# Low weight parts by an adding transfer in place of a GpSimd subtraction, and low products last in each unit

## The reference

```
for l in range(2):
    h = rmsnorm(x, norm_g[l])
    u_a, z_a, u_b, z_b, q, z_x, g_a, g_b, g_x = split(h @ w_in[l])     # 1024 x 7168
    y_a = s5_branch(u_a) ; y_a = y_a * sigmoid(y_a @ w_glu + b_glu)
    o_a = (y_a * silu(z_a)) @ w_br_ssm
    c_b = silu(layernorm(conv31(u_b[:, :512] * sigmoid(u_b[:, 512:]))))
    o_b = (c_b * silu(z_b)) @ w_br_conv
    o_x = (attention(q, memory) * silu(z_x)) @ w_br_xatt
    m = sigmoid(g_a) * o_a + sigmoid(g_b) * o_b + sigmoid(g_x) * o_x
    x = x + m @ w_out
y = rmsnorm(x, final_norm_g)
```

## Time and profile before

| | us |
|---|---|
| median of 3 runs | 1299.31 (1298.57 to 1300.8) |
| profiled execution, device time | 1295.11 |
| profiled execution, span of its instructions | 1293.3 |
| TensorE busy | 1163.0 (90%), 8322 matmuls |
| VectorE busy | 833.9 (64%) |
| ScalarE busy | 395.3 (31%) |
| GpSimd busy | 387.6 (30%), of which L555 366.0 |
| DMA engines, mean busy share | 37.5% |

### The profile page before, as it was taken

The page is one execution under the profiler, slowest core; times in us unless marked ns, Lnnn a source line. Parts: engine busy times, 40 slices in busy tenths (PEclk is TensorE's granted clock), DMA queues, the critical chain, the costliest instruction groups (busy, mean ns, idle before and its releaser), DMA issues.

```text
span 1293.3 us, 19959 instructions
## 1 busy us (share of the span) xinstructions
PE 1163.0 (90%) x8322; PEld 1068.3 (83%) x8322; DVE 833.9 (64%) x1223; ACT 395.3 (31%) x556; POOL 387.6 (30%) x183
## 2 busy tenths in 40 slices
PE   5997999979788987989999979999979798979995
PEld 4497989579788987989977968868969798969995
DVE  1889964888779860457825995757857887233322
ACT  4331433142242423223214234233314241312212
POOL 0144234233231432133321522322343222304340
PEclk8998999999897998989999989999989799989998
DMA  7563235732121255154334623547221214422442
GB/s 202 164 226 99 63 115 158 139 88 65 53 82 33 66 121 132 38 134 158 108 99 133 210 64 99 179 126 111 82 68 54 62 35 119 98 66 87 132 131 66
DMA packets 205808, 137.94 MB, mean 107 GB/s; under 512 B 45842, under 2 KB 186570, under 8 KB 204934
## 3 DMA queue, kind: packets, MB, share of 16 engines
q1 hardware_dynamic: 205574, 135.61, 37.5%
q10 hardware_dynamic: 144, 1.05, 0.2%
HBM read 121.86 MB, written 15.72 MB: 106 GB/s over the span
## 4 chain that ended last, share of the span: by engine, by line
PE 67%; DVE 19%; DMA 4%; ACT 3%; SPq 3%; issue 2%; POOL 1%; DVEq 0%; ACTq 0%
PE acc L635 46%; DVE cacc L1363 9%; PE acc L676 4%; PE acc L981 3%; PE mp L831 2%; PE mp L888 2%; PE mp L600 2%; PE mp L764 1%; DMA w_st<-in_w_in 1%; DVE X L1357 1%; PE mp L690 1%; POOL w_lo L555 1%; DVE t L1357 1%; PE mp L805 1%; PE mp L855 1%
## 5 line engine op out<-in xcount | busy, mean ns | idle before, releaser
L555 POOL TENSOR_TENSOR w_lo<-w_st,w_hi 128x1024 fp32r<-128x1024 f32 x144 | 366.0, 2542 | 852.3 <-ACT w_hi L1068 852.0
L635 PE MATMUL acc<-h_hi,w_hi 128*128 128x260 f32 x1664 | 345.4, 289 | 7.6 <-DVEq L1691 7.6
L1068 ACT CAST w_hi<-w_st 128x1024 fp32r<-128x1024 f32 x144 | 150.9, 1048 | 643.7 <-PE acc L635 602.0
L635 PE MATMUL acc<-h_lo,w_hi 128*128 128x260 f32 x1664 | 337.4, 285 | 0.0
L635 PE MATMUL acc<-h_hi,w_lo 128*128 128x260 f32 x1664 | 337.2, 285 | 0.0
L635 PEld LDWEIGHTS acc<-h_hi,w_hi 128*128 128x128 f32 x1664 | 260.6, 191 | 14.5 <-issue 10.0
L635 PEld LDWEIGHTS acc<-h_hi,w_lo 128*128 128x128 f32 x1664 | 259.1, 190 | 0.0
L635 PEld LDWEIGHTS acc<-h_lo,w_hi 128*128 128x128 f32 x1664 | 258.9, 190 | 0.0
L1363 DVE SCALAR_TENSOR_TENSOR cacc<-vx,cw,cacc 128x512 f32<-128x512 f32 x232 | 220.1, 1019 | 3.0 <-DVE xT L1357 1.5
L635 PE MATMUL acc<-bh,w_hi 128*128 128x260 f32 x384 | 85.7, 307 | 32.4 <-ACTq L1201 13.2
L635 PEld LDWEIGHTS acc<-bh,w_hi 128*128 128x128 f32 x384 | 64.9, 207 | 35.6 <-issue 17.3
(11 more groups left out here) (276 smaller groups left out, 1481.4 us busy)
## 6 DMA issues: line engine op xcount, KB each, us to landing
w_st<-in_w_in SPq DMA_DIRECT2D x104, 512.0 KB, 3.9
kb<-in_cache_mem_k SPq DMA_DIRECT2D x16, 512.0 KB, 5.7
kb<-in_cache_mem_v SPq DMA_DIRECT2D x16, 512.0 KB, 4.1
w_st<-in_w_out SPq DMA_DIRECT2D x16, 512.0 KB, 4.1
x_scratch<-xT SPq DMA_DIRECT2D x8, 520.0 KB, 6.8
xT<-x_scratch SPq DMA_DIRECT2D x4, 1040.0 KB, 8.0
kvw<-in_w_k SPq DMA_DIRECT2D x8, 512.0 KB, 6.5
kvw<-in_w_v SPq DMA_DIRECT2D x8, 512.0 KB, 3.6
```

Of the source, the lines that this page charges most:

```text
L555: pool.tensor_tensor(w_lo[:, n % 2, :], w_st[:, n % 2, :], w_hi[:, n % 2, :].bitcast(F32), ALU.subtract).then_inc(w_staged_free, 1)
L635: last = pe.matmul(acc_ps[acc][:, a, 0:HC], w_of(w, slot, k), x_of(x, k, a), start=(k == 0 and p == 0), stop=(k == kts - 1 and p == 2))
L1068: act.copy(w_hi[:, n % 2, :], w_st[:, n % 2, :]).then_inc(w_hi_done, 1)
```

## The change

`w_lo` is made in another way and used at another time.

- ACT, right after it rounds `w_hi`, waits for that copy and writes its negative into `w_lo` (a second pass over 128 x 1024).
- GpSimd no longer computes. It issues a transfer that adds `w_st` onto `w_lo` in SBUF, so that `w_lo` holds `w_st - w_hi`. The landing is told by one semaphore for each slot, `w_lo_done[0]` and `w_lo_done[1]`.
- SP's next load into the slot waits for that landing.
- TensorE begins a unit when `w_hi` is there (`w_hi_done`). It does all products with `w_hi` first, and those with `w_lo` last, behind a wait for the landing.

```
-            w_staged_free = sem("w_staged_free")
+            w_lo_done = [sem(f"w_lo_done{i}") for i in range(2)]
             w_hi_done = sem("w_hi_done")
+            w_neg_done = sem("w_neg_done")
...
             def ring_load(l, src, i, width=P):
                 n = l * UNITS + i
-                sp.wait_ge(w_staged_free, n + 1)
+                if n >= 2:
+                    sp.wait_ge(w_lo_done[n % 2], 16 * (n // 2))
                 sp.dma_start(w_st[:, n % 2, :]...).then_inc(w_loaded[n % 2], 16)
...
-            pool.sem_inc(w_staged_free, 2)
...
                 def low(name, first, end):
-                        pool.wait_ge(w_hi_done, n + 1)
-                        pool.tensor_tensor(w_lo[:, n % 2, :], w_st[:, n % 2, :], w_hi[:, n % 2, :].bitcast(F32),
-                                           ALU.subtract).then_inc(w_staged_free, 1)
+                        pool.wait_ge(w_neg_done, n + 1)
+                        pool.dma_start(w_lo[:, n % 2, :], w_st[:, n % 2, :], accum_op=ALU.add).then_inc(w_lo_done[n % 2], 16)
...
-            def products(l, slot, acc, name, i, terms, kts, x_of, w_of, tiles_done=None):
+            def products(l, n, acc, name, i, high, low, kts, w_of, tiles_done=None):
+                pe.wait_ge(w_hi_done, n + 1)
                 wait(pe, l, f"acc_free{acc}", use[name] + i + 1)
                 for k in range(kts):
                     if tiles_done:
                         wait(pe, l, tiles_done, k + 1)
-                    for p, (w, x) in enumerate(terms):
+                    for x in (high, low):
                         for a in range(2):
-                            last = pe.matmul(acc_ps[acc][:, a, 0:HC], w_of(w, slot, k), x_of(x, k, a),
-                                             start=(k == 0 and p == 0), stop=(k == kts - 1 and p == 2))
+                            pe.matmul(acc_ps[acc][:, a, 0:HC], w_of(w_hi, n % 2, k), x[:, k, a, :],
+                                      start=(k == 0 and x is high), stop=False)
+                pe.wait_ge(w_lo_done[n % 2], 16 * (n // 2 + 1))
+                for k in range(kts):
+                    for a in range(2):
+                        last = pe.matmul(acc_ps[acc][:, a, 0:HC], w_of(w_lo, n % 2, k), high[:, k, a, :],
+                                         start=False, stop=(k == kts - 1))
                 last.then_inc(acc_ready[acc], 1)
...
     in high(n), on ACT:
                     act.copy(w_hi[:, n % 2, :], w_st[:, n % 2, :]).then_inc(w_hi_done, 1)
+                    act.wait_ge(w_hi_done, n + 1)
+                    act.activation(w_lo[:, n % 2, :], w_hi[:, n % 2, :].bitcast(F32), ACT.Copy, scale=-1.0).then_inc(w_neg_done, 1)
```

More of the change, by code:

```diff
@@ L640, in tile_w @@
                 return w[:, slot, k * P:(k + 1) * P]
-            def tile_x(x, k, a):
-                return x[:, k, a, :]
             def in_unit(l, name, i, tiles_done=None):
                 n = l * UNITS + unit[name] + i
-                pe.wait_ge(w_staged_free, n + 3)
-                products(l, n % 2, i % 2, name, i // 2, ((w_hi, h_hi), (w_lo, h_hi), (w_hi, h_lo)), KT, tile_x, tile_w, tiles_done)
+                products(l, n, i % 2, name, i // 2, h_hi, h_lo, KT, tile_w, tiles_done)
             def gate(l, name, j):
                 n = l * UNITS + unit[name] + j // 2 * 3 + j % 2
-                pe.wait_ge(w_staged_free, n + 3)
-                products(l, n % 2, j % 2, name, j // 2 * 2, ((w_hi, h_hi), (w_lo, h_hi), (w_hi, h_lo)), KT, tile_x, tile_w)
+                products(l, n, j % 2, name, j // 2 * 2, h_hi, h_lo, KT, tile_w)
             def branch(l, name, j, ready):
                 n = l * UNITS + unit[name] + j // 2 * 3 + 2
-                pe.wait_ge(w_staged_free, n + 3)
                 low = {"gx": q_r[:, :, :, :], "gb": cv_r[:, :, 0, :, 0:HC], "ga": q_r[:, :, :, :]}[name]
-                high = bh[:, :, :, :]
-                products(l, n % 2, j % 2, name, j // 2 * 2 + 1, ((w_hi, high), (w_lo, high), (w_hi, low)), ET, tile_x,
+                products(l, n, j % 2, name, j // 2 * 2 + 1, bh[:, :, :, :], low, ET,
                          lambda w, slot, k: w[:, slot, (k * 2 + j % 2) * P:(k * 2 + j % 2 + 1) * P], ready if j == 0 else None)
@@ L997, in _ @@
                     n = l * UNITS + unit["out"] + i
-                    pe.wait_ge(w_staged_free, n + 3)
-                    products(l, n % 2, i % 2, "out", i // 2, ((w_hi, m_hi), (w_lo, m_hi), (w_hi, m_lo)), KT, tile_x, tile_w,
+                    products(l, n, i % 2, "out", i // 2, m_hi, m_lo, KT, tile_w,
                              "m_done" if i == 0 else None)
```

## The result

The changed kernel takes 1346.94 us (median; 1336.46 to 1354.13), beside 1298.94 us for the kernel before on the same chip: the ratio is 1.036, with a 95% interval of 1.029 to 1.044. The forecast was 1321 us. It is slower, as forecast, and the median lies in the range of 1302 to 1350 us, but the loss is 48 us where 22 were forecast.

A forecast was written before the change was run, and what follows sets the result against it. TensorE's idle time, mostly waits for DVE, which GpSimd's subtraction slows, was taken as what is left to gain. 1293.3 - 47 + 9 + 4 + 56 = 1315.3 us of span, 1321 us device time; range 1302 to 1350, 8 in 10 1266 to 1390.

The forecast's parts named there:

- DVE's relief: Without GpSimd's subtraction DVE runs at its free pace and TensorE's waits for it shrink: -47 us (-30 to -55).
- ACT's second pass: 1.13 us a pass with handover, counted in full at eight places with the rounding on the chain: +9 us (0 to 14).
- low products last: Where blocks arrive one by one, more matmuls follow the last block on TensorE: +4 us (0 to 10).
- transfer and ring: `w_st` is held until the adding transfer lands; a slot's turn of 13.2 us exceeds TensorE's 11.5 us: +56 us.
- the lateness of a pair: Each pair of units in the weight ring comes 1.65 us late, for 34 pairs: +56 us.
- which wait binds: The ring binds first, at A + L over 9.2 us; the low products' wait allows A to 7.3, branch groups 5.4 us.
- A and L: Lengths of the adding transfer (A) and the load into its slot (L), collisions included: taken as 6.4 and 4.5 us.
- The slope: In the ring, 1 us more of adding transfer or load costs 34 us, more if looser pairs join.
- What was to show it: Taps about 0.73 us, DVE under 780 us, no waits at L764 and L929, transfer over 5.2 us with roundings awaiting loads.
- Rivals 1 and 2: First: transfer hidden, DVE's relief stays, device 1273 us, chance 0.35. Second: relief and ring lateness cancel, 1299 us, chance 0.08.
- Rival 3: The ring binds hard: transfer 8 us, load 5 us, some 42 pairs 3.8 us late, device 1425 us; chance 0.13.
- Rival 4: DVE isn't freed, since writing a transfer's descriptors takes the port shared with GpSimd: -47 shrinks to -10, device 1310 us; chance 0.07.

The follow-up runs named there:

- the floor: The kernel before with GpSimd's subtraction replaced, from the third unit on, by a memset of 8 columns: 1237.8 us, ratio 0.948.
- nothing_plus_both: The kernel before with an 8-column memset for GpSimd's subtraction, plus ACT's second pass and low products last, no transfer: 1249.2 us, ratio 0.962.
- the doses: The changed kernel with its adding transfer cut to 64 columns (1262.7 us) or 512 columns (1281.9 us), or made a full-size plain copy (1280.3 us).
- the negative first: The changed kernel with ACT's passes exchanged: negative straight from `w_st`, then rounding; SP's next load also waits for the rounding: 1320.9 us, ratio 1.012.
- copy and addition: The changed kernel with its transfer as a plain copy that adds nothing, 1280.3 us, beside the changed kernel itself, 1346.9 us.
- relief_only: The kernel before with GpSimd's subtraction cut to 8 of 1024 columns from the third unit on: 1242.7 us, ratio 0.958.

## Why the prediction was right and wrong, point by point

The terms, as the runs give them one on top of the other (times in us):

| term | forecast | measured | from |
|---|---|---|---|
| DVE's relief | -47 | -61.5 | 1299.3 to 1237.8 |
| ACT's second pass | +9 | +15.6 | 1237.8 to 1253.4 |
| low products last | +4 | -4.2 | 1253.4 to 1249.2 |
| transfer and ring | +56 | +97.7 | 1249.2 to 1346.9 |
| sum | +22 | +47.6 | |

The same steps by the pages of the profiled executions, split into the time in which TensorE stood idle (span less busy time) and its busy time, with the same 8322 matmuls throughout:

| term | span | TensorE idle | TensorE busy |
|---|---|---|---|
| DVE's relief | -57.3 | -40.8 | -16.5 |
| ACT's second pass | +15.2 | +8.3 | +6.9 |
| low products last | -6.4 | -0.9 | -5.5 |
| transfer and ring | +103.8 | +72.2 | +31.6 |
| sum | +55.3 | +38.8 | +16.5 |

- **What bounds the kernel** was read rightly: the DVE and GpSimd exclusion is real, and its removal alone is nearly all of the largest gain that any run here showed.
- **Relief.** The waits went much as said. On the floor L764 lost all of its 14.7 us (forecast 14.7), L929 8.5 (forecast 10), and L1682, L1809, L1201, L1691 and the state products (L888) together 20.6 us (forecast 22 for the group). In the changed kernel L764 kept 3.3 and L929 6.5 us, so neither vanished as the prediction's last part wanted. What passed the bound of -55 is TensorE's busy time: 16.5 us less. The prediction named the clock as a reason for its outer bound and gave it no size. The taps had also lost more than the 51 us read from them: undisturbed, 29 take 19.30 us, and their busy time fell by 64 us (220.1 to 156.0).
- **Second pass.** Mechanism right, size low: outside the range of 0 to 14. The idle time rose by 8.3 us, close to the 9 forecast; the other 6.9 us are busy time again.
- **Order.** +5 on the kernel before, as forecast; about -4 where it counts.
- **The ring, the step that failed.** The prediction made 34 pairs of units 1.65 us late each, +56 us, and the runs give +98. Three parts of that step were wrong: the lateness of a pair, which wait binds, and the clock.
- **The lateness of a pair.** The turn in the dense stretch is 14.6 us, not 13.2: the addition has a mean of 6.8 us there against the 6.4 assumed, the fixed part 2.5 against 2.3, and the rest is ACT waiting for TensorE, which itself came late. So a pair is 3.0 us late, not 1.65. And A and L are no constants: in q the cache loads stand beside the ring, one load took 10.43 us and the transfers before and beside it 8.5 and 8.9, and two pairs lost 9.3 us in each layer. Measured against nothing_plus_both, the loss lies in q (9.3 and 9.2), ga (17.9 and 11.9), out (4.7 and 12.4) and gx (4.9 and 8.5).
- **Which wait binds.** The prediction said that the ring binds first and that the wait ahead of the low products is looser. TensorE waited there 25 times, 40.1 us, and never for a rounded copy. In 15 of the 25 (24.8 us) ACT's rounding had not waited for its load: the slot was in time, and the transfer alone outlasted the matmuls in front of the wait. Ten of the 25 (20.5 us) are w_br units, with 16 matmuls in front. For these the prediction had a limit of 5.4 us, which its own A of 6.4 passed, and gave them no term. The worst in layer 1, ga's ninth unit (in order of ACT, GpSimd and SP):

```profile
1233.47 1.05 ACT L1067 CAST w_hi<-w_st 128x1024 fp32r<-128x1024 f32 x1 [3.61 <-PE acc L642]
...
1235.90 0.86 POOL L556 DMA_DIRECT2D w_lo<-w_st  x1 [4.89 <-ACT w_lo L1069]
...
1235.96 0.58 SPq L521 DMA_DIRECT2D xT<-x_scratch  x1
```

Its load had landed at 1232.40 us, and the rounding began when TensorE had ended the unit two before. The transfer then took 9.64 us, beside a load and the 1040 KB for `xT`, and TensorE stood for 4.49 us. In the `out` units, where the chain above runs, the loads were late. No run takes the two waits apart, since the doses and the negative first shorten both; how much of the 98 us is the ring's own stays open.

- **The clock**, for which the term had nothing. Of the 104 us between nothing_plus_both and the changed kernel in the profiled executions, 32 are busy time. The granted clock fell from 0.960 to 0.937 of full speed over the span; 118 us of TensorE's busy time lay at the lower level, against 63 us, and matmuls take nearly twice as long there (2.10 against 1.11 us above), so as an estimate 26 to 28 of the 32 us are the clock.
- **The slope held.** The prediction put 1 us of transfer at 34 us of time; the runs give 67 us for the 2.1 us between copy and addition, 32 us for 1 us, and 26 us for the 1.05 us of the negative first. Since both waits shorten together, this does not speak for the ring alone.
- **Two errors that cancelled in part.** The other three terms came to -50 where -34 was forecast. With the ring alone mis-sized, the time would have been 16 us further off. That the median lies in the forecast's range is in part this luck.
- **What was to show it.** Taps and DVE's busy time (660 us, under 780) came out, and so did a median landing over 5.2 us with ACT waiting for `w_st` loads (243 us). The wait at the low products, which was to speak against the forecast if it stood in every unit, stood in 25 places. As a sign it was ill chosen: the low part lands 1.4 us and the whole transfer after the rounded copy, so a late ring too shows at the low products, as in the `out` units.
- **Rivals.** Rivals 1 and 2 fall, though rival 1's A of 4.9 was not absurd: the shortest landing is 4.5 us. Rival 3's A of 8 us occurs, but only in 15 of 144 transfers. Rival 4 falls: taps at 746 ns beside 144 transfers, and 29 taps in 19.30 us while one was issued (at 85.74 us), as long as in relief_only.
- **The rule weighed.** The Trainium skill (Collectives: The Full Stack, The bandwidth ceiling) says that a reducing transfer goes at half the rate, and the trace agrees for this one inside a core: 2.83 against 1.50 us of the engines. The estimate of 4.4 us from it, with the Trainium skill's DMA: Bandwidth & Descriptors (Anatomy of one DMA), is the landing of a transfer with nothing beside it (4.5 us at best, and in the median of the 29 such ones). What the estimate lacked was the other streams.

## What to carry to other kernels

A transfer in place of an engine's work is free only while two sums have room: the buffers' turn (load, each pass, handovers, transfer), and the way from the rounding to the landing against the matmuls in front of the wait, unit kind by unit kind. Use durations under collision, and count a wait on TensorE with the slow clock behind it: here 72 us of idle time came with 32 us of longer busy time. Before replacing a step everywhere, find where the engine that it frees is really waited for: here the transfer in 25 of 72 units, with the negative first, gains 30 us, and in all 72 it gives a loss of 48 (21 with the negative first). A measured median of a transfer hides what decides; look at the longest ones and at what is issued beside them.

## What the runs showed of the hardware

- An adding transfer from SBUF to SBUF on GpSimd's queue, 128 x 4 KB: landing 4.5 us at best, 5.5 in the median, 10.8 at most (the last beside a ring load and four cache loads); 2.83 us of all 16 engines; GpSimd holds 0.87 us for its issue. The plain copy: 2.8 us at best, 3.4 in the median, 1.50 us of the engines, 0.53 us of GpSimd.
- DVE can keep GpSimd out: beside the same 29 taps in a row one operation of GpSimd on eight columns that reads two tensors took 0.25 us, and the next 11.05 us. A memset took 0.11 us in the same place. In the kernel before it was DVE that was slowed. Which of the two gives way changed with small shifts in time; why was not settled.
- After a wait of 2.33 us TensorE ran at 1.2 GHz for some 3 us, which nearly doubled the wait's price.
- The same matmuls kept TensorE busy for 1147.9 us at a mean granted clock of 0.960 and for 1179.5 us at 0.937.
